# Two-layer hybrid encoder trunk: output copies of one delta-rule pair set ahead of a convolution, weight splits set behind the next pair's decays, one small tile padded

## The reference

```python
h = rmsnorm(x, even_norm_mix)
dn_qkv, dn_a, dn_b, dn_gate, fq, fk, fv = split_cols(h @ even_w_in, IN0_SPLITS)
dn_qkv = silu(causal_dwconv(dn_qkv, even_dn_conv))          # kernel width 4
...
q = l2norm(q) * dk ** -0.5; k = l2norm(k)                   # per head, 128 features
gcum = cumsum(g within a chunk); decay = exp(gcum_i - gcum_j), lower triangle
Lmat = strict_lower(beta * (k k^T) * decay) + I
u, w = triangular_solve(Lmat, [v * beta, k * beta * exp(gcum)])
for each chunk: v_new = u - w S; o = q_dec S + qk v_new; S = S * g_last + k_dec^T v_new
o_a = rmsnorm(o, even_dn_norm) * silu(dn_gate)
```

## Time and profile before

| | |
|---|---|
| time, median of 3 runs | 1417.47 us (1417.21 to 1417.5) |
| the profiled execution's own time | 1416.82 us |
| its span (first to last instruction) | 1415.1 us |
| PE busy | 1359.9 us (96%) |
| DVE busy | 816.3 us (58%) |
| ACT busy | 574.7 us (41%) |
| mean granted TensorE clock | 0.975 of full speed |

### The profile page before, as it was taken

How to read it: one execution, slowest core, us unless ns; L and a number is a source line. 1 busy time by engine, 2 the same in 40 slices (tenths; PEclk the granted TensorE clock), 3 DMA queues, 4 the chain that set the end, 5 groups by cost and what they waited for, 6 DMA issues and landing times.

```text
span 1415.1 us, 21106 instructions
## 1 busy us (share of the span) xinstructions
PE 1359.9 (96%) x7795; PEld 1098.5 (78%) x7795; DVE 816.3 (58%) x1260; ACT 574.7 (41%) x794; POOL 124.0 (9%) x137
## 2 busy tenths in 40 slices
PE   7989989999899999999999999999999999999996
PEld 5868768777678888888888777777878888888885
DVE  4886675777656654355555555555656653355543
ACT  5522411465434452233334455554444442233342
POOL 1030030001121000000012001000210000000011
PEclk9999799999999999999999999999999999999998
DMA  8311010223235523333224332332323423433131
GB/s 257 90 45 48 15 47 1 75 57 119 71 107 162 154 74 89 104 112 96 67 78 127 90 82 69 91 88 74 90 60 94 113 67 93 125 95 96 56 93 59
DMA packets 218666, 124.93 MB, mean 88 GB/s; under 512 B 6063, under 2 KB 215450, under 8 KB 218356
## 3 DMA queue, kind: packets, MB, share of 16 engines
q1 hardware_dynamic: 213760, 112.52, 28.4%
q0 software_dynamic: 3664, 11.58, 2.9%
q10 hardware_dynamic: 1188, 0.08, 0.1%
HBM read 119.92 MB, written 9.48 MB: 91 GB/s over the span
## 4 chain that ended last, share of the span: by engine, by line
PE 88%; DVE 6%; ACT 3%; issue 1%; DMA 1%; ACTq 0%; POOL 0%; DVEq 0%; POOLq 0%
PE acc L699 72%; PE acc L1108 3%; PE R L977 2%; PE R L991 2%; PE R L831 2%; PE R L721 2%; DVE cta L1656 1%; PE R L1081 1%; ACT wh L416 1%; PE R L819 1%; PE R L1040 1%; PE R L880 1%; DVE wl L420 1%; DVE wl L1665 1%; DMA out<-ob 0%
## 5 line engine op out<-in xcount | busy, mean ns | idle before, releaser
L699 PE MATMUL acc<-mh,wh 128*128 128x512 f32 x1120 | 319.2, 405 | 3.3 <-ACT wh L1271 1.8
L699 PE MATMUL acc<-ml,wh 128*128 128x512 f32 x1120 | 313.3, 398 | 3.1 <-DVE ml L1582 3.1
L699 PE MATMUL acc<-mh,wl 128*128 128x512 f32 x1120 | 309.6, 396 | 0.1
L420 DVE TENSOR_TENSOR wl<-raw,wh 128x2048 fp32r<-128x2048 f32 (+1 forms) x103 | 222.1, 2156 | 118.2 <-ACT wh L416 118.2
L416 ACT ACTIVATE wh<-raw 128x2048 fp32r<-128x2048 f32 (+1 forms) x111 | 200.6, 1807 | 141.7 <-PE acc L699 141.7
L699 PEld LDWEIGHTS acc<-mh,wh 128*128 128x128 f32 x1120 | 207.4, 190 | 56.6 <-issue 12.0
L699 PEld LDWEIGHTS acc<-ml,wh 128*128 128x128 f32 x1120 | 211.7, 191 | 50.2 <-DVE ml L1582 4.6
L699 PEld LDWEIGHTS acc<-mh,wl 128*128 128x128 f32 x1120 | 211.8, 191 | 45.4 <-DVE wl L436 0.5
L565 POOL TENSOR_TENSOR ssum<-ssum,sq 128x512 f32<-128x512 f32 x32 | 49.9, 1559 | 747.1 <-ACT sq L1221 746.4
L2145 DVE SCALAR_TENSOR_TENSOR cta<-cb,pv,cta 128x512 f32<-128x512 f32 x88 | 66.1, 751 | 74.1 <-ACT cta L1520 67.7
L699 PE MATMUL acc<-ah,wl 128*128 128x512 f32 x352 | 98.0, 396 | 0.0
(11 more groups left out here) (314 smaller groups left out, 1544.2 us busy)
## 6 DMA issues: line engine op xcount, KB each, us to landing
raw<-in_ffn_w_in SPq DMA_DIRECT2D x88, 512.0 KB, 5.0
raw<-in_ffn_w_out SPq DMA_DIRECT2D x32, 384.0 KB, 4.0
raw<-in_even_w_in SPq DMA_DIRECT2D x23, 512.0 KB, 5.2
raw<-in_ffn_w_out SPq DMA_DIRECT2D x32, 320.0 KB, 3.7
raw<-in_odd_w_qkv SPq DMA_DIRECT2D x16, 512.0 KB, 4.6
rel_bias_extended<-rel_bias_rows POOLq DMA_DIRECT2D x16, 320.0 KB, 4.0
raw<-in_even_w_out SPq DMA_DIRECT2D x8, 512.0 KB, 4.7
raw<-in_odd_w_qkv SPq DMA_DIRECT2D x16, 256.0 KB, 3.1
```

Source lines behind the costliest of these rows:

```text
L420: nc.vector.tensor_tensor(wl[s][:, 0:n], raw[s][:, 0:n], wh[s][:, 0:n].bitcast(F32), ALU.subtract).then_inc(sem(f"w_tail{s}"), 1)
L699: last = nc.tensor.matmul(acc[2 * s + t][:, :], ws[0 if form[0] else 1][:, t, k, :], mov[0 if form[1] else 1][:, k, :], start=form == HEAD ...
```

## The change

It has five parts. In pair 0, DVE copies the outputs `o` out of the banks directly after the last block of the loop, ahead of the convolution of k of head 3, which stood between them. In pair 0 the two halves of weight split 1 no longer follow at once; they are taken in pair 1 behind the decays (`"decays": 2`), for which the two DVE generators become one. In pair 1 the same edit of the loop sets the last piece (the second half of a weight split) behind `rope(0)` and the output copies. On PE, pair 1 now also gives 8 units between `gcol` and `sq_c`, as pair 0 does, and the later gives `(4, 4, 4, 4, 4, 4)` become `(3, 3, 3, 3, 2, 2)`, so that the sum stays 24. And `pick` is allocated as 32 floats, which moves every tile behind it by 96 bytes in each partition (for instance `xin`, `oh` and `ah` from 147232 to 147328).

```diff
-        pick = sb("pick", [P, 8])
+        pick = sb("pick", [P, 32])[:, 0:8]
...
-                if p == 0:
-                    give(fill, 8)
+                give(fill, 8)
                 for h in (0, 1):
                     pe.wait_ge(sem(f"sqk{h}"), p + 1)
...
-                g = ((2, 2, 2, 2, 2, 2), (4, 4, 4, 4, 4, 4))[p]
+                g = ((2, 2, 2, 2, 2, 2), (3, 3, 3, 3, 2, 2))[p]
...
-                    piece(b)
+                    if b < NB - 2:
+                        piece(b)
                 if p:
                     rope(0)
                 for h in (0, 1):
                     r = full(dve, ph, f"o{h}", 0)
                     free(V.tensor_copy(d[h]["os"], r[:, :]), ph, f"o{h}", 0)
+                piece(NB - 2)
                 piece("o")
...
-            dn_pair(0, chained(first, vg_evac(0), qk_evac(1)),
+            evacs = chained(first, vg_evac(0), qk_evac(1), vg_evac(1), first_attention())
+            dn_pair(0, evacs,
...
-                     "Y32": 1, "X32": 1, "Y64": 1, "X64": 1, "u": 1, 0: 1, 2: 2, "o": 2})
-            dn_pair(1, chained(vg_evac(1), first_attention()),
-                    {"kh": 1, "N": 1, ...
+                     "Y32": 1, "X32": 1, "Y64": 1, "X64": 1, "u": 1, 0: 1, 2: 2})
+            dn_pair(1, evacs,
+                    {"decays": 2, "kh": 1, "N": 1, ...
```

More of the change, by code:

```diff
@@ L1979, in first_attention @@
                 yield from half_splits(0, UNIT["diff"] + 1)
-            dn_pair(0, chained(first, vg_evac(0), qk_evac(1)),
+            evacs = chained(first, vg_evac(0), qk_evac(1), vg_evac(1), first_attention())
+            dn_pair(0, evacs,
                     {"decays": 2, "kh": 1, "N": 1, "qh": 1, "qk": 1, "ktok": 1, "c2": 2, "cU1": 1, "cU2": 1, "cU3": 2, "cX": 1,
-                     "Y32": 1, "X32": 1, "Y64": 1, "X64": 1, "u": 1, 0: 1, 2: 2, "o": 2})
-            dn_pair(1, chained(vg_evac(1), first_attention()),
-                    {"kh": 1, "N": 1, "qh": 1, "qk": 1, "ktok": 1, "c2": 2, "cU1": 1, "cU2": 1, "Y32": 1,
+                     "Y32": 1, "X32": 1, "Y64": 1, "X64": 1, "u": 1, 0: 1, 2: 2})
+            dn_pair(1, evacs,
+                    {"decays": 2, "kh": 1, "N": 1, "qh": 1, "qk": 1, "ktok": 1, "c2": 2, "cU1": 1, "cU2": 1, "Y32": 1,
                      0: 1, 1: 1, 2: 1})
```

## The result

The changed kernel takes 1402.8 us (median of 4 runs, 1398.58 to 1403.33), the kernel before beside it 1417.34 us. The ratio is 0.9892, 95% interval 0.9873 to 0.9912: 15.3 us less, between 12.5 and 18.0 (the two medians differ by 14.5). The prediction said 1413.1 us and at best 1410.0. The profiled execution took 1403.33 us (span 1401.6).

A forecast was written before the change was run, and what follows sets the result against it. PE's own work was taken to set the end, with DVE and ACT setting the pace early in pair 1. Terms -4.5 + 0.1 = -4.4 us took the median from 1417.47 to 1413.1 us, range 1410.0 to 1416.5.

The forecast's parts named there:

- `pick`, set to 0 with bounds of 0.5 us: Moving tiles behind `pick` by 96 bytes was taken as worth 0, within 0.5 us either way.
- The removed wait: Passage from pair 0 to 1: earlier output copies end PE's 2.55 us wait at `grow`; sums of squares end at 156.73.
- The clock behind the sums: After pair 1's sums of squares: one half-clock drop of about 3.4 us, costing nothing further.
- -4.5 us at `post_out`: Pair 1: DVE starts `post_out` near 167.6 instead of 172.13, and `ktok` follows at 187.4 instead of 191.87.
- rival 1: Low clock lasts through pair 1's output sums, `ro` comes near 170; gain only 2 us, 1415.5; chance 0.20.
- the forecast branch: Start of pair 1: only one short low-clock stretch, `post_out` near 167.6; gain 3.0 to 5.5 us; chance 0.57.
- rival 2: PE's whole time comes back: gain 9.5 us, 1408.0, or in part 5.5 to 9; chance 0.13 with its parts.
- The waits behind it: Pair 1, PE: `rq` waits about 1.4 us for DVE, `ktok` about 4.5 instead of 2.2 for ACT; end unaffected.
- The splits at no cost: Two 1.18 us split halves moved behind pair 1's decays fill a DVE wait and cost nothing; up to 2.4 uncovered.
- The 8 units, "cover what the sums wait for": Filler ahead of pair 1's sums of squares, 5.58 us, covers the wait for head 1's squares of k, near 151.
- End of pair 1, 0.1 us: Second half split behind the output copies: `wl` ready at 252.3, first read at 252.23; cost 0.1 us, bounds 0 and 1.2.
- the 4.4 us of the forecast: Total predicted gain: 4.5 us at the start of pair 1 less 0.1 us at its end.

The follow-up runs named there:

- e1: The kernel before with only the padded `pick` tile, old order of work; 1405.41 us, ratio 0.9919.
- e5: The whole changed kernel run once more, unaltered; 1401.98 us, ratio 0.9892 to the kernel before.
- e2: The whole change without the padded `pick` tile, so the new order alone; 1410.53 us, ratio 0.9958 to the kernel before.
- e9: The whole change with the weight tiles moved to 32 bytes past a multiple of 128; 1431.95 us, ratio 1.0119 to the kernel before.
- e13: The whole change with `mh`, `ml` and the weights all 32 bytes past a multiple of 128; 1428.39 us, ratio 1.0074 to the kernel before.
- e14: The whole change with only the weights moved, to 64 bytes past a multiple of 128; 1423.18 us, ratio 1.0048 to the kernel before.
- e8: The whole change with 6 filler units instead of 2 ahead of `ktok`; 1404.82 us, ratio 0.9913 to the kernel before.
- e6: The kernel before plus padded tile and the earlier output copies only; 1409.53 us, ratio 0.9942.
- e11: The kernel before plus padded tile and the splits behind the decays only; 1405.58 us, ratio 0.9917.
- e7: The whole change with the old gives of pair 1; 1400.22 us, ratio 0.9879 to the kernel before.
- e4: The kernel before plus padded tile, with `mh` and `ml` alone moved 32 bytes past a multiple of 128; 1423.98 us, ratio 1.0052.
- e3: The kernel before with `pick` of 16 floats, so tiles behind it start 64 bytes past a multiple of 128; 1412.07 us, ratio 0.9979.

## Why the prediction was wrong, point by point

**`pick`, set to 0 with bounds of 0.5 us: the step that failed.** It read "both take 396 ns" from the earlier trace rows and concluded from the two means that a start off 128 bytes costs nothing. The mean for `mh` held rows at the half clock, the one for `ah` none; the medians were 389 and 397 in the same trace. The term measures -10.4 us by the spacings and -11.5 us by e1's ratio (-8.9 to -14.0). No rival held it either, so this one comparison of unlike means put the time below the range. The forecast lies 10.3 us above the measured median, about the size of this term. The Trainium skill ("SBUF — State Buffer", section "Operand start alignment") asks of a start only a multiple of the element's size and says that it speaks of legality, not speed; both addresses fulfil it, and it sets no price for the term. The runs here show one: 7 ns a matmul.

**The removed wait: right.** No wait of `grow`, copies at 144.61 (said 144.3), sums ended at 157.17 (156.7).

**The clock behind the sums, and with it -4.5 us at `post_out`: mis-sized in the profile that counts.** Taken was one drop of 3.4 us; the stretch lasted 10.24 us, and `post_out` stood at 171.15, not 167.6, `ktok` at 190.91, not 187.4. That is rival 1, given 0.20. The execution e5 of the same kernel took the forecast branch, with `post_out` at 167.28 us:

```profile
143.52 0.61 PE L953 MATMUL R<-dn_qkD,vn 128*128 128x128 f32 x4
...
159.92 2.36 PE L721 MATMUL R<-cst,dn_A 128*128 128x1 f32 x16
...
187.02 1.11 PE L829 MATMUL R<-cst,dn_kh 128*128 128x128 f32 x8 [4.25 <-ACT dn_A L1364]
```

Here the half clock lasted 3.41 us (157.24 to 160.65), and the distance to `ktok` is 43.5 us, 4.6 less than before. So the step's arithmetic held, on its condition. Behind `ktok` that execution even gained more, as a part of rival 2 has it: by 300 us it was 7.6 us ahead of the kernel before. Of six traces with the change's order as it stands (the change, e5, e2, e9, e13, e14), five have the long stretch and 46.6 to 46.7 us, a gain of 1.4 to 1.6; only e5 has the short one (e8, the same up to `kk`, has 6.83 us). The chances of forecast and rival 1 at this place were the wrong way round. Why an execution takes one or the other I did not settle: the same instructions stand there, in e5 0.7 us earlier.

**The waits behind it: right.** `rq` waits 0.84 us (said 1.4), `ktok` 4.22 (said 4.5).

**The splits at no cost: right in cost, wrong in meaning.** They were priced as a neutral move. e6 and e11 show that they carry the order edit: by the traces the copies without them lose 1.2 us to `ktok`, and they win none without the copies.

**The 8 units, "cover what the sums wait for": they do, but by the traces they cost more than they cover.** With the old gives the sums wait 1.3 us; the 8 units take 5.56 us (148.12 to 153.68). Counted from pair 0's last output product, ACT's roots for the outputs stand 1.8 us later with them than in e7 (19.40 beside 17.59 us; 19.42 in e5). e7's distance to `ktok` is 4.5 us shorter than the whole change's and 1.3 us shorter than e5's, and the kernel has the lowest medians of all (1399.95 and 1400.22). (The order of PE is the old one only from the give behind `ktok` on, not from the fifth give on: ahead of `ktok` the filler has 6 matmuls more than before.) By its ratios (0.9879 and 0.9889, both against 0.9892) it can't be told from the whole change.

**End of pair 1, 0.1 us: right.** PE's row that needs the tail, against the earlier trace rows, starts at 250.31, 1.03 us after the one at 249.28 where 0.91 is the usual step.

```profile
249.28 1.07 PE L699 MATMUL acc<-ml,wh 128*128 128x512 f32 x4
250.31 1.19 PE L699 MATMUL acc<-mh,wl 128*128 128x512 f32 x4
```

**The rest of the sum: near the forecast in part by luck.** By the traces the span fell by 13.5 us, of which 10.4 are the spacing. The other 3 are not the order's in this execution. Each instruction compared with itself, this execution is 2.05 us ahead at 220 us and level with the kernel before at 280 to 334 us, behind a stretch at half clock from 257.65 to 261.06 that the trace of before does not have. The gain then rises to 4.95 us at 430. Most of that is the clock: between 360 and 420 us before has 13.66 us at half clock, after has 3.41. The order of the work there is the same in both, and e1, with the old order, has 10.24 us there; e4 and e11, whose output copies are the old ones, have the stretch near 258 too. So such stretches move from one execution to the next. The order's gain at 300 us was 0.0 in this execution, 2.1 in e2's, 7.6 in e5's; by the medians it is worth 5.9 us alone (e2, 4.2 to 7.8), and the 4.4 us of the forecast lie within that. The scatter of a kernel goes with the clock: e11's fastest execution (1397.89 us) has a mean clock of 0.984, its slowest (1407.72) 0.978.

## What to carry to other kernels

Look at where each TensorE operand starts in its partition, moving and stationary alike, and pad a small tile so that the large ones behind it start on a multiple of 128 bytes; this was worth more than the hand-made order (11.5 us beside 5.9, each alone). Compare durations of two groups by their medians, or at one clock: a mean over half-clock and full-clock rows makes unlike things look alike. Before a copy is set ahead in a queue, follow what it pushes back to the next engine that waits there: here the copies paid only once the splits had left the same queue.

## What the runs showed of the hardware that I had not expected

- A 512-column float32 matmul (one of the three products of a split) follows the last one after 227 ns when both operands start on a multiple of 128 bytes, and after 233 to 234 ns in the mean when either starts 32 bytes past one (230 to 238 within `ah`'s stream). This holds at the full clock. A multiple of 256 is not needed: `ah` at 147328 (1151 times 128) has the 227 ns. At half clock the spacing is 427 ns for `mh` and `ml`, on a multiple (e1) or 32 bytes past one (e4).
- 64 bytes past: 233 ns, nearly constant, for a moving operand (`ah`, e3); for the weights 233 to 234 ns with `mh` but 229 with `ah` (e14). Why the two streams differ there is open.
- Two operands off cost no more than one (232.7 beside 233.4 ns in the mean, e13), and a distance between the operands that is a multiple of 128 bytes does not help.
- The granted clock stood at 0.50 for 10.24 us in which PE was busy for 10.06, and in another execution of the same kernel for 3.41 us at the same place.
